# Two 256-token feed-forward stages: gate and up by seven block products on streamed weights, modulation panels through a side buffer

## What is computed

```python
D_MODEL = 1024
D_FF = ((8 * D_MODEL // 3 + 255) // 256) * 256      # 2816

def _swiglu(h, w_in, w_out):
    g, u = jnp.split(h @ w_in, 2, axis=-1)
    return (jax.nn.silu(g) * u) @ w_out
...
    cond = jax.nn.silu(c)
    for i in range(DEPTH):
        mod = cond @ ada_w[i] + ada_b[i]
        sh1, sc1, g1, sh2, sc2, g2 = [m[:, None, :] for m in jnp.split(mod, N_MOD, axis=-1)]
```

## Time and profile before

| | us |
|---|---|
| median of 3 runs (lowest, highest) | 2280.93 (2278.07, 2282.87) |
| span of the profiled execution | 2282.1 |
| TensorE busy | 2206.5 (97%) |
| VectorE busy | 1081.8 (47%) |
| ScalarE, GpSimd busy | 437.9, 127.6 |
| stage 1, gate and up (1024.4 to 1184.2) | 159.8 |
| stage 1, down (1185.2 to 1261.9) | 76.7 |

### The profile page before, as it was taken

The page is one execution under the profiler, slowest core; times in us unless marked ns, Lnnn a source line. Parts: engine busy times, 40 slices in busy tenths (PEclk is TensorE's granted clock), DMA queues, the critical chain, the costliest instruction groups (busy, mean ns, idle before and its releaser), DMA issues.

```text
span 2282.1 us, 38552 instructions
## 1 busy us (share of the span) xinstructions
PE 2206.5 (97%) x16511; PEld 1597.5 (70%) x16511; DVE 1081.8 (47%) x2086; ACT 437.9 (19%) x1029; POOL 127.6 (6%) x127
## 2 busy tenths in 40 slices
PE   7999999999999999999999989999999899999998
PEld 4444453478886787678888768888786677777776
DVE  5477765578888335854450453442144341111112
ACT  1321071200000003640000261000133131101001
POOL 0210030000000420000000000000003000000000
PEclk9999999999999999999999999999999799999999
DMA  8524542244544334027886315888443147999996
GB/s 293 176 95 148 183 142 74 74 148 152 194 171 123 91 101 158 1 75 258 294 267 180 141 64 172 291 292 230 158 160 128 37 160 289 372 376 370 380 379 253
DMA packets 308647, 436.36 MB, mean 191 GB/s; under 512 B 12020, under 2 KB 167283, under 8 KB 308235
## 3 DMA queue, kind: packets, MB, share of 16 engines
q1 hardware_dynamic: 303412, 422.55, 54.3%
q0 software_dynamic: 2144, 7.21, 0.9%
q10 hardware_dynamic: 2934, 4.31, 0.5%
HBM read 429.01 MB, written 4.93 MB: 190 GB/s over the span
## 4 chain that ended last, share of the span: by engine, by line
PE 92%; DVE 5%; ACT 1%; issue 1%; DMA 0%; ACTq 0%; SPq 0%; DVEq 0%
PE banks L656 78%; PE banks L916 3%; PE banks L665 1%; DVE mem L1922 1%; ACT mem L3009 1%; PE banks L1060 1%; PE banks L1480 1%; DVE mem L1918 1%; PE banks L1095 1%; DVE mem L1925 1%; DVE mem L2525 1%; PE banks L880 1%; PE banks L1073 1%; PE banks L1102 0%; DMA mem<-in_ctx 0%
## 5 line engine op out<-in xcount | busy, mean ns | idle before, releaser
L656 PE MATMUL banks<-mem 128*32 128x128 f32 (+5 forms) x12738 | 1827.2, 359 | 20.8 <-ACT mem L3009 8.7
L656 PEld LDWEIGHTS banks<-mem 128*128 128x128 f32 (+3 forms) x12738 | 1309.2, 148 | 503.4 <-issue 296.5
L1922 DVE SCALAR_TENSOR_TENSOR mem<-mem 128x512 f32<-128x512 f32 (+5 forms) x539 | 383.5, 739 | 22.0 <-DMA mem<-mem 7.6
L3009 ACT ACTIVATE mem<-banks 128x512 f32<-128x512 f32 (+9 forms) x347 | 138.8, 422 | 1095.8 <-PE banks L656 785.9
L3009 ACT ACTIVATE mem<-mem 128x256 f32<-128x256 f32 (+10 forms) x447 | 193.1, 481 | 636.1 <-DVE mem L1922 468.8
L1922 DVE SCALAR_TENSOR_TENSOR mem<-banks,mem 128x256 f32<-128x256 f32 (+7 forms) x250 | 130.7, 546 | 327.2 <-PE banks L656 225.8
L1925 DVE TENSOR_TENSOR mem<-mem,banks 128x256 f32<-128x256 f32 (+3 forms) x88 | 43.2, 491 | 416.2 <-ACT mem L3009 389.2
L1925 DVE TENSOR_TENSOR mem<-banks,mem 128x256 f32<-128x256 f32 (+4 forms) x320 | 123.2, 387 | 186.1 <-PE banks L656 135.2
L1925 DVE TENSOR_TENSOR mem<-mem 128x256 f32<-128x256 f32 (+12 forms) x275 | 150.9, 561 | 34.8 <-ACT mem L3009 19.8
L665 PE MATMUL banks<-mem 128*128 128x128 f32 (+2 forms) x393 | 59.5, 288 | 21.1 <-DMA mem<-in_ctx 11.5
L665 PEld LDWEIGHTS banks<-mem 128*128 128x128 f32 (+2 forms) x393 | 44.5, 148 | 50.4 <-issue 25.3
(11 more groups left out here) (197 smaller groups left out, 779.2 us busy)
## 6 DMA issues: line engine op xcount, KB each, us to landing
mem<-in_ada_w SPq DMA_DIRECT2D x96, 1024.0 KB, 9.7
mem<-in_moe_w_gate_up SPq DMA_DIRECT2D x64, 1024.0 KB, 10.8
mem<-in_ffn_w_in SPq DMA_DIRECT2D x44, 1024.0 KB, 6.4
mem<-in_moe_w_down SPq DMA_DIRECT2D x48, 768.0 KB, 10.2
mem<-in_moe_w_gate_up SPq DMA_DIRECT2D x32, 768.0 KB, 12.6
mem<-in_ffn_w_out SPq DMA_DIRECT2D x32, 704.0 KB, 6.6
mem<-in_ffn_w_gate_up SPq DMA_DIRECT2D x22, 1024.0 KB, 6.4
mem<-in_ab_w_in SPq DMA_DIRECT2D x16, 1024.0 KB, 10.0
```

Source lines behind the costliest of these rows:

```text
L656: ins = nc.tensor.matmul(o, lhsT, rhs, start=start, stop=stop)
L1922: return V.scalar_tensor_tensor(out=o, in0=a, scalar=sc, in1=b, op0=op0, op1=op1)
L3009: ac = lambda o, i, f, **k: nc.scalar.activation(o, i, f, **k)
```

## The change

In stages 1 and 2 (the first gate/up panel, i = 0, stays as it was) each of the ten other panels is taken as a 2 x 2 block product: token tiles of 128 by halves of the features, halves of the features by gate and up. Now the *tokens* are loaded into the array and the 256 columns of *weights* stream. Seven products of four matmuls replace 32 matmuls. VectorE makes three token sums once (`s1`, `s2`, `s4`, then `s3` in place), four weight sums a panel (`t1`, `t2`, one in place, `t4`), and five sums of product banks (`add`). The result has tokens on the partitions, so TensorE turns it by four transposes a panel (`turn_act`, into `PS[3]`) and ScalarE copies it to `act`.

The twelve modulation panels leave the ring. GpSimd's queue loads them in halves of 1 MB (`side[0]`, `side[1]`, one buffer each). Half 0 of the next chunk is asked for when VectorE has used the fourth row block (`dve_for_dma`), half 1 when it has used the eighth (`acc_ready`). Five chunks are summed beside gate and up, four steps a panel; the other seven, eight steps each, ahead of `add_out` of the first seven down panels, and TensorE's `side_sum` stands behind each of these. Some semaphores are merged under new names elsewhere (`down_copied` is `act_copied`, `floor_cleared` is counted in `strip_made`); their waits are the same.

```diff
@@ tables and tiles
-MOE_FIRST = 139
+MOE_FIRST = 115
-FFN_FIRST = (23, 59, 97)
+FFN_FIRST = (23, 59, 85)
...
+        class TokenBlocks:
+            def __init__(self, stage):
+                self.stage, self.at, self.first = stage, stage - 1, FFN_FIRST[stage]
+                self.act = work(0, KF, L)
...
+                self.t = [[work(14592 + 3072 * j + 1024 * i, 4, L) for i in range(3)] for j in range(2)]
+                self.s1, self.s2, self.s4 = (hT[:, 4 * a:4 * a + 4, L + P * b:L + P * b + P] for a, b in ((0, 0), (0, 1), (1, 0)))
+                self.s3 = self.tokens(1, 0)
+                self.a, self.b, self.c, self.e, self.d = (PS[i][:, 0:L] for i in (6, 7, 0, 1, 2))
+                self.turned = PS[3]
...
+        def weight_part(w, half, up):
+            return w[:, 4 * half:4 * half + 4, L * up:L * up + L]
+        side = [work(5632 + 2048 * i, 4, T2) for i in range(2)]
+        SIDE_CHUNKS = 5
@@ SyncE queue
+            def ffn_tokens(w_in, w_out):
+                assert panels.n in FFN_FIRST[1:], panels.n
+                for i in range(11):
+                    gu_panel(w_in, i, FF)
+                v = w_out.rearrange("(k p) n -> p k n", p=P)
+                for m in range(8):
+                    load(KF, P, [(slice(a, a + 11), slice(0, P), v[:, a:a + 11, m * P:m * P + P]) for a in (0, 11)])
@@ TensorE
+            def side_sum():
+                await_("acc_ready", "acc")
...
+                for a in range(4):
+                    last = mm(quarter(bank, 0, a), const("ones")[:, 0:32], columns(acc_t[:, 0, :], a))
+                last.then_inc(s["ada_ready"], 1)
+            def token_products(tb, i):
+                w = panel(8, 512)
+                t1, t2, t4 = tb.t[i % 2]
...
+                if i > 1:
+                    pe.wait_ge(s["blk_silu"], tb.after("blk_silu", i - 1, 1))
+                product(tb.a, tb.tokens(0, 0), weight_part(w, 0, 0)).then_inc(s["blk_act"], 1)
+                if i == 1:
+                    pe.wait_ge(s["gu_taken"], c["gu"].n + 2)
+                    pe.wait_ge(s["blk_tokens"], tb.tokens_made(2))
+                else:
+                    pe.wait_ge(s["blk_taken"], tb.after("blk_taken", i - 1, 1))
+                pe.wait_ge(s["blk_sums"], tb.after("blk_sums", i, 2))
+                product(tb.b, tb.s2, t2).then_inc(s["blk_ready"], 1)
+                if i > 1:
+                    pe.wait_ge(s["blk_taken"], tb.after("blk_taken", i - 1, 2))
+                product(tb.c, tb.s1, t1).then_inc(s["blk_ready"], 1)
+                if i == 1:
+                    pe.wait_ge(s["blk_tokens"], tb.tokens_made(4))
+                else:
+                    pe.wait_ge(s["blk_taken"], tb.after("blk_taken", i - 1, 5))
+                pe.wait_ge(s["blk_sums"], tb.after("blk_sums", i, 3))
+                product(tb.e, tb.s3, weight_part(w, 0, 1)).then_inc(s["blk_ready"], 1)
+                pe.wait_ge(s["blk_copied"], tb.after("blk_copied", i, 1))
+                product(tb.a, tb.tokens(0, 1), weight_part(w, 1, 0), more=True).then_inc(s["blk_act"], 1)
+                if i > 1:
+                    turn_act(tb, i - 1)
+                    pe.wait_ge(s["blk_taken"], tb.after("blk_taken", i - 1, 4))
+                product(tb.d, tb.s4, weight_part(w, 1, 1)).then_inc(s["blk_ready"], 1)
+                pe.wait_ge(s["blk_taken"], tb.after("blk_taken", i, 3))
+                pe.wait_ge(s["blk_sums"], tb.after("blk_sums", i, 4))
+                product(tb.e, tb.tokens(1, 1), t4, more=True).then_inc(s["blk_ready"], 1)
+            def turn_act(tb, i):
+                pe.wait_ge(s["dve_for_turn"], tb.after("dve_for_turn", i, 1))
...
+                for b in range(2):
+                    for t in range(2):
+                        last = turn(tb.turned[:, b * L + t * P:b * L + t * P + P], tb.tok[:, t, b * P:b * P + P])
...
+                for i in range(1, 11):
+                    token_products(tb, i)
+                    if i % 2 == 0:
+                        side_sum()
+                pe.wait_ge(s["blk_silu"], tb.after("blk_silu", 10, 1))
+                pe.wait_ge(s["blk_taken"], tb.after("blk_taken", 10, 2))
+                for m in range(8):
+                    w = panel(KF, P)
+                    bank = out_item()
+                    for k in range(KF):
+                        if (m, k) == (0, 12):
+                            turn_act(tb, 10)
+                        if (m, k) == (0, 20):
+                            pe.wait_ge(s["act_copied"], tb.after("act_copied", 10, 1))
+                        last = mm(bank[:, 0:L], w[:, k, :], tb.act[:, k, :], k == 0, k == KF - 1)
+                    last.then_inc(s["out_ready"], 1)
+                    if m < 12 - SIDE_CHUNKS:
+                        side_sum()
@@ VectorE
+            def side_steps(tb, j, first, end):
+                for k in range(first, end):
+                    if k % 4 == 0:
+                        dve.wait_ge(side_loaded[k // 4], 16 * (12 * tb.at + j + 1))
+                    if k == 4:
+                        dve.wait_ge(s["dve_for_dma"], 1 + 12 * tb.at + j + 1)
+                    elif k:
+                        dve.wait_ge(s["acc_step"], c["astep"].n)
+                    w, cc = side[k // 4][:, k % 4, :], conds[:, 2, k:k + 1]
+                    if k == 0:
+                        last = V.tensor_scalar(acc_t[:, 0, :], w, cc, None, ALU.mult)
+                    else:
+                        last = stt(acc_t[:, 0, :], w, cc, acc_t[:, 0, :])
+                    if k == 3:
+                        last.then_inc(s["dve_for_dma"], 1)
+                    elif k == 7:
+                        last.then_inc(s["acc_ready"], 1)
+                    else:
+                        last.then_inc(s["acc_step"], 1)
...
+                    if part == 0:
+                        dve.wait_ge(panel_loaded[m % NSLOT], (m // NSLOT + 1) * 32)
+                        ins = tt(t1, weight_part(w, 0, 1), weight_part(w, 0, 0), ALU.subtract)
+                    elif part == 1:
+                        dve.wait_ge(s["blk_sums"], tb.after("blk_sums", i, 1))
+                        ins = tt(t2, weight_part(w, 1, 1), t1, ALU.subtract)
+                    elif part == 2:
+                        ins = tt(weight_part(w, 0, 1), weight_part(w, 1, 1), weight_part(w, 0, 1), ALU.subtract)
+                    else:
+                        dve.wait_ge(s["blk_sums"], tb.after("blk_sums", i, 2))
+                        ins = tt(t4, weight_part(w, 1, 0), t2, ALU.subtract)
+                    ins.then_inc(s["blk_sums"], 1)
...
+                def made(i):
+                    dve.wait_ge(s["blk_silu"], tb.after("blk_silu", i, 2))
+                    if i > 1:
+                        dve.wait_ge(s["pe_for_copy"], tb.after("pe_for_copy", i - 1, 1))
+                    tt(tb.tok, tb.gate, tb.up).then_inc(s["dve_for_turn"], 1)
+                for i in range(1, 11):
+                    j, k = (i - 1) // 2, 4 * ((i - 1) % 2)
+                    if i > 1:
+                        add(tb.gate[:, 1, :], tb.e, tb.v, tb.after("blk_ready", i - 1, 5))
+                        if k == 0:
+                            ada(bias, 1 - par, j - 1, 1)
+                    weight_sum(i + 1, 0)
+                    if i > 1:
+                        made(i - 1)
+                    side_steps(tb, j, k, k + 1)
+                    dve.wait_ge(s["blk_copied"], tb.after("blk_copied", i, 1))
+                    add(tb.v, tb.b, tb.m1, tb.after("blk_ready", i, 1))
+                    weight_sum(i + 1, 1)
+                    side_steps(tb, j, k + 1, k + 2)
+                    add(tb.w, tb.c, tb.v, tb.after("blk_ready", i, 2))
+                    weight_sum(i + 1, 2)
+                    side_steps(tb, j, k + 2, k + 3)
+                    add(tb.up[:, 1, :], tb.e, tb.w, tb.after("blk_ready", i, 3))
+                    weight_sum(i + 1, 3)
+                    side_steps(tb, j, k + 3, k + 4)
+                    add(tb.up[:, 0, :], tb.d, tb.w, tb.after("blk_ready", i, 4))
+                add(tb.gate[:, 1, :], tb.e, tb.v, tb.after("blk_ready", 10, 5))
+                ada(bias, 1 - par, SIDE_CHUNKS - 1, 1)
+                made(10)
+                c["panels"].n += 19
+                for m in range(8):
+                    j = SIDE_CHUNKS + m
+                    if j < 12:
+                        side_steps(tb, j, 0, 8)
+                    add_out(par, 1, 1, m)
+                    add_square(m, L, hT)
+                    if j < 12:
+                        ada(bias, 1 - par, j, 1)
@@ GpSimd queue
+            for at in range(2):
+                pool.wait_ge(s["att_taken"], (16, 24)[at])
+                w = A["ada_w_2"][at].rearrange("(k p) n -> p k n", p=P)
+                for j in range(12):
+                    for half in range(2):
+                        if j and half == 0:
+                            pool.wait_ge(s["dve_for_dma"], 1 + 12 * at + j)
+                        elif j:
```

(5 more changed lines are left out.)

162 lines of the change are left out of this document (125 added, 37 removed).

## The result

The changed kernel takes 2251.99 us (median of 4 runs, 2250.54 to 2252.94) against 2280.31 for the kernel before, a ratio of 0.9873 (0.986 to 0.9886): 28.3 us faster. The forecast was 2265, with a range from 2252 to 2288. The direction was right. The size was not: the time is 2 us under that of the first rival (2254, nothing stalls) and a hundredth of a microsecond outside the range.

The account below looks back on a forecast made before the run. TensorE, busy 97% of the span, was taken as the bound. From 2282.1 us, 26.5 saved in both stages and 10.6 of side buffer stalls gave 2266.2, less 1.2 to a median of 2265; range 2252 to 2288.

Parts of the forecast that it names:

- the first rival: Side buffer in the down part: loads land in under 7.2 us, nothing stalls; 2255.6 us profiled, 2254 median; chance 0.17.
- Fewer matmuls: Gate and up, stages 1 and 2: 4 matmuls fewer, four transposes more; net 1.22 us a panel, 12.2 a stage.
- The wait ahead of the down part: TensorE's 1.05 us wait for the last gate/up product's store, ahead of the down part, goes in each stage.
- VectorE beside gate and up: VectorE's new work, 22.9 us per two panels, fits under TensorE's 25.7; 0 us stall taken.
- The chain of the side buffer: Down part: half 1's load and four steps follow in turn, so chunks may come slower than TensorE's 10.05 us panel beat.
- L: Time of a 1 MB side buffer load from issue on GpSimd's queue to landing; up to 6.92 us is hidden.
- the formula for the stall: Down part's stall per stage: 6 x (L - 6.92) - 2.4 us.
- What is L?: Step estimating the down part's load landing: 5.1 us from below, 7.8 with 2.7 of issue, 12.2 fully queued; took 8.2.
- The stall term: TensorE's waits for side buffer chunks in the down parts: 5.3 us a stage, 10.6 us in both.
- The base: Whole kernel: medians taken as 1.2 us under the profile's sums, which start from 2282.1 us.
- The second: Down part: slow side buffer loads eat the gain; L = 9.5 cancels it, L = 11 gives 2299; chance 0.09 beyond 10.
- The third: Gate and up: GpSimd's issuing of loads stops VectorE, 13 us a stage more, median 2291; chance 0.10, alone or in part.

Follow-up runs that it names:

- the side buffer alone: Kernel before with only the modulation panels moved to GpSimd's queue in the changed kernel's order, gate and up with 32 matmuls a panel: 2280.80 us against 2281.14, ratio 0.9998.
- the runs with held-up loads: Changed kernel with one or two GpSimd memsets of 128 x 2048 ahead of each half for chunks 6 to 11: 2285.23 us and 2307.77 us.
- a third place: Changed kernel with three 1 MB places for the side buffer's halves instead of two: 2250.33 us; with GpSimd also held up by two shorter memsets a load, 2250.85 us.

## Why the prediction was right or wrong

**Fewer matmuls: right.** Products with exchanged roles follow each other every 1.73 us, as the earlier trace rows had it. Four transposes cost 0.43 and not 0.51: I had noted both and kept the wrong one, since the 0.51 from the earlier trace rows has in it a pause ahead of the next instruction. That is 0.08 x 20 = 1.6 us in both stages. 13.2 + 0.8 = 14.0 us a stage is what stage 2 shows.

**The wait ahead of the down part: right.** The 1.05 us is gone in after and is there again with the side buffer alone.

**VectorE beside gate and up: right.** No wait of TensorE for it. VectorE was busy 104 us of the 143.2 of gate and up, the first panel included, where my 22.3 per two panels makes 111 for the ten alone: the sum was high, on the safe side.

**The chain of the side buffer: right as a mechanism, wrong in one term.** The loop, the period L + 3.13 against 10.05, and the formula for the stall are what the runs with held-up loads and with a third place show; with the landings measured there (7.9 us and the hold) the formula gives stage 1's growth within 0.3 us. The step that failed is "What is L?". I took 8.2 and measured 7.2 and 6.7. The 2.7 us of issue, scaled from 0.51 us for 192 KB by bytes, was 0.75: GpSimd's issue hardly grows with the size. In the gate and up parts, at a DMA share of 0.70, a load lands after 5.5 to 5.8 us in stage 1 and 5.5 to 6.4 in stage 2; the 1.0 to 1.6 us on top in the down parts came with the fuller transfer engines (0.93), where I had allowed 0.4. So two errors of opposite sign, and the wrong one was the larger. The stall term was 10.6 us; measured were 1.6 and 0.5. The formula with L = 7.2 gives 0; with the 0.30 us between a step's end and the next issue, which it leaves out, it gives 1.1. Single late loads (up to 8.9 us, just ahead of the two waits) make it vary from execution to execution.

The Trainium skill, DMA: Bandwidth & Descriptors, "Anatomy of one DMA — SWDGE (gpsimd) path", gave an estimate of 4.4 us for L; the least landing in the stretches read here is 5.4. Its number was further off than mine, but its conclusion, no stall, was nearly right.

**The base: off by 0.6 us.** The step from the profile's sum to a median was 1.2 us, the span of 2282.1 less the median of three runs. A fourth run moved that median to 2280.31, which makes it 1.8 us. The sentence that the profiled execution was 1.2 us above the runs' median was wrong beside this, since it compared a span with a time: a run's time is some 1.9 us more than its span (after: 2251.44 and 2249.5), so that execution took about 2284.0 us, 3.7 over the median and above all four runs.

**The sum again:** 2282.1 - 26.5 - 1.6 + 0.5 to 1.6 - 1.8 = 2252.7 to 2253.8, within 2 us of the 2251.99 measured. From 2265.0: 9.0 to 10.1 us are the term of L, 1.6 the transposes, 0.6 the base; the other 0.7 to 1.8 is of the size of the spread of executions.

**The rivals.** The first is what happened, but for waits of 0.5 to 1.6 us. The second, the other side, is real and was near: with half 1 issued 2.16 us after its place is free, 1.9 us later than in after, L was 10.1 with the hold, over my point of 9.5, and the whole gain is gone (ratio 1.002). The third fell: steps of 749 ns and sums of 1216 ns beside GpSimd's loads are the 0.78 and 1.22 of the earlier trace rows. The Trainium skill, SBUF — State Buffer, "Who interferes with whom", had ruled it out, and the rows agree with it.

**The range.** Its lower end was rival 1 with cheap transposes; with the base of 1.8 us that is 2252.2. It left no room below for the spread of measurements, although I had put what a measurement can tell at 4.6 us. That the time fell just outside and not just inside is chance; that it fell near the end and not near 2265 is the term of L. The chance of 0.17 for rival 1 was too low: its bound, L under 7.2, lay between the least measured landing of such a size, 5.1, and a value of which 2.7 us were a proportion that no row supported.

## What to carry to other kernels

A fixed cost must not be scaled by bytes from one small transfer: put both ends, all fixed and all proportional, into the range, and see on which side of the threshold each lies. Where a buffer with one place per item closes a loop of landing and use, compare the period with the beat. Here they were near each other (10.3 to 10.6 us against 10.05), and a third place of half a panel took the loop off the path: 1.9 us of delay cost 33 us with two places, and 1.6 us of delay cost 0.5 us with three. Take the landing of the load that closes the loop, under the traffic of that loop, and not the median of all loads. Compare a span with a span and a time with a time. Where TensorE waits long for such a loop, its matmuls behind the wait are slow too, but they cost only where no further wait of the loop follows (3 us here, at the end of a stage).

## What the runs showed of the hardware

- GpSimd needs 0.75 us to issue a load of 1 MB in 2 KB rows, against 0.51 us for 192 KB.
- Such a load lands after 5.5 to 5.8 us in stage 1's gate and up part (5.5 to 6.4 in stage 2's) with the transfer engines at a share of 0.70, after 7.2 us (5.9 to 8.9) at 0.93. A second load in flight (three places) left the median at 7.2.
- In the down parts with held-up loads, behind waits of TensorE of 1.99 to 5.89 us, the 52 records of a panel took 11.6 to 13.1 us where 10.12 is usual (once, behind 3.42 us, they took 10.12), with a granted clock of 0.50 in the 5 us behind a wait of 5.14 us. Behind waits up to 1.82 us they took 10.12. Stage 1 still grew by the loop's 16.2 us and no more.
- At the head of a stage the clock can fall behind short waits: behind the same last wait of 1.27 us the granted clock over 6 us was 0.72 in one execution and 1.00 in another, and 96 records took 1.7 us more.
